# First expert pass of a product-key layer: 112 candidate sums per head for 256, token tiles weighed one by one, one-hot batches over experts 33 to 116

## The reference

```python
q = (xt @ w_query).reshape(n, 8, 2, 128)              # 8 heads, 2 halves
s = jnp.einsum('nhpd,hpkd->nhpk', q, sub_keys)        # 128 keys per half
s1, i1 = lax.top_k(s[:, :, 0], 16)
s2, i2 = lax.top_k(s[:, :, 1], 16)
cand = (s1[..., :, None] + s2[..., None, :])          # 16 x 16 sums per head
cidx = (i1[..., :, None] * 128 + i2[..., None, :])
top, pos = lax.top_k(cand, 16)                        # 16 experts per head
gates = jax.nn.softmax(top)
act = gelu(x . expert_u[e]);  y = sum(gate * act * expert_v[e])
```

## Time and profile before

| | |
|---|---|
| median of 3 runs (lowest, highest) | 1992.9 us (1984.32, 1996.92) |
| profiled execution: time, span | 1994.66 us, 1992.9 us |
| mean granted TensorE clock | 0.952 |
| busy: PE, PEld, DVE, ACT, POOL | 1835.5, 1774.0, 1564.3, 650.6, 931.9 us |
| first pass, L1137: 3072 matmuls | 686.4 to 1388.6 |
| second pass, L1157: 3072 matmuls | 1391.2 to 1971.0 |
| second-level search on DVE begins | 704.3 |
| first gather, last dot | 740.0, 1384.0 |
| first and last matmul of the gate batches | 1004.8, 1311.3 |
| HBM read, written | 361.28 MB, 62.06 MB |

### The profile page before, as it was taken

One profiled execution on the slowest core, in us unless ns is written; L12 is line 12 of the kernel. 1 busy time (PEld: TensorE's weight loads), 2 busy tenths in 40 slices (PEclk: granted clock), 3 DMA queues, 4 the chain that ended last, 5 costly groups with the idle time before them and its releaser, 6 DMA issues.

```text
span 1992.9 us, 29861 instructions
## 1 busy us (share of the span) xinstructions
PE 1835.5 (92%) x11654; PEld 1774.0 (89%) x11654; DVE 1564.3 (78%) x2754; ACT 650.6 (33%) x1037; POOL 931.9 (47%) x676
## 2 busy tenths in 40 slices
PE   5999567887989999999889999997999999999998
PEld 4999566765989999899889999997999999999997
DVE  4797777755459989999899999944788888888852
ACT  4443211112133332222333434432333333333332
POOL 2899897000000258788756566665133334333200
PEclk9999698865989999999999999998999999999999
DMA  7221100001552258787569999999899999999841
GB/s 203 70 77 51 37 1 0 1 1 39 151 170 75 71 173 286 249 275 268 199 205 303 305 304 297 302 333 384 293 364 395 346 364 351 354 344 363 316 172 35
DMA packets 192957, 424.87 MB, mean 213 GB/s; under 512 B 11236, under 2 KB 119296, under 8 KB 184617
## 3 DMA queue, kind: packets, MB, share of 16 engines
q1 hardware_dynamic: 155505, 287.99, 41.9%
q0 software_dynamic: 37312, 134.97, 19.5%
HBM read 361.28 MB, written 62.06 MB: 212 GB/s over the span
## 4 chain that ended last, share of the span: by engine, by line
PE 64%; DVE 26%; issue 3%; DMA 2%; POOL 2%; ACT 2%; SPq 0%; DVEq 0%; ACTq 0%
PE psum L1157 29%; PE psum L1137 14%; PE psum L827 7%; PE psum L1125 4%; PE psum L822 3%; PE psum L915 2%; DMA rowg<-in_expert_u_rows,idx 2%; DVE sel L1938 1%; DVE eqa L1935 1%; DVE junk L1960 1%; DVE cT L1611 1%; DVE besti L1887 1%; DVE WR L1540 1%; DVE sring L1891 1%; PE psum L973 1%
## 5 line engine op out<-in xcount | busy, mean ns | idle before, releaser
L1137 PE MATMUL psum<-xT,WS 128*128 128x416 f32 x3072 | 607.4, 357 | 21.8 <-POOL WS L764 21.4
L1137 PEld LDWEIGHTS psum<-xT,WS 128*128 128x128 f32 x3072 | 580.1, 191 | 30.7 <-POOL WS L764 25.1
L1157 PE MATMUL psum<-AR,WS 128*128 128x416 f32 x3072 | 579.8, 351 | 2.6 <-DVE AR L2048 2.6
L1157 PEld LDWEIGHTS psum<-AR,WS 128*128 128x128 f32 x3072 | 575.0, 188 | 7.5 <-DVE AR L2048 3.0
L764 POOL TENSOR_TENSOR WS<-RAWP,WS 128x1024 fp32r<-128x1024 f32 x128 | 311.7, 2437 | 496.9 <-ACT WS L1438 495.9
L757 POOL DMA_INDIRECT rowg<-in_expert_v,idx x128 | 177.5, 1386 | 315.2 <-DVE acc L1973 305.6
L827 PE MATMUL psum<-xT,WR 128*128 128x280 f32 (+1 forms) x1968 | 261.3, 296 | 2.7 <-DVE xT L1566 2.7
L827 PEld LDWEIGHTS psum<-xT,WR 128*128 128x128 f32 x1968 | 258.4, 193 | 3.4 <-DVE xT L1566 3.2
L1448 ACT ACTIVATE WS<-RAWP 128x1024 fp32r<-128x1024 f32 x128 | 135.8, 1061 | 348.1 <-PE psum L1157 335.5
L2041 DVE TENSOR_TENSOR WS<-RAWP,WS 128x1024 fp32r<-128x1024 f32 x128 | 156.6, 1224 | 117.6 <-ACT WS L1448 117.6
L1475 ACT ACTIVATE actA<-psum 128x416 f32<-128x416 f32 x128 | 66.3, 518 | 447.8 <-PE psum L1137 411.9
(11 more groups left out here) (326 smaller groups left out, 1937.9 us busy)
## 6 DMA issues: line engine op xcount, KB each, us to landing
RAWP<-in_expert_u SPq DMA_DIRECT2D x64, 1024.0 KB
RAWP<-in_expert_v SPq DMA_DIRECT2D x64, 1024.0 KB
act_dram<-actA SPq DMA_DIRECT2D x128, 208.0 KB
gate_dram<-gblk SPq DMA_DIRECT2D x13, 2048.0 KB, 11.9
Gt<-gate_dram SPq DMA_DIRECT2D x32, 832.0 KB
act<-act_dram SPq DMA_DIRECT2D x64, 416.0 KB
RAW<-in_w_in SPq DMA_DIRECT2D x8, 1024.0 KB, 5.4
RAW<-in_w_query SPq DMA_DIRECT2D x8, 1024.0 KB, 5.6
```

The costliest lines, as they stand in the source:

```text
L1137: last = mm(bank[e % 2][:, 0:TD], ws(e)[:, pw, kt * P:(kt + 1) * P], xT[:, px, kt, TSP:TPE], start=(kt == 0 and i == 0), stop=(kt == KT - ...
L1157: last = mm(bank[dt][:, 0:TD], ws(NK + e)[:, pw, dt * P:(dt + 1) * P], AR[:, e % 4, pa, :], start=(e == 0 and i == 0), stop=(e == NK - 1 a ...
```

## The change

The candidates: the best 4 keys of the first half are still summed with all 16 of the second; the other 12 only with the best 4 of the second half, 64 + 48 = 112 sums, since a pair (a, b) can be among the 16 best only if (a + 1)(b + 1) is at most 16. The keys of the picks are found otherwise: the position is turned into an ordinal for each half, compared (greater or equal) with the first ordinal of each of 16 keys, times the step from key to key, and added up in a tree, all in bf16, both halves at once. Its temporaries move: `eqa` into columns of `xT` that the first pass does not read, `sel` into `wrow` (so that the last norm's weights are loaded in the second pass), `stepb` and `topa` into old masks.

Order: tiles 0, 1 and 2 are searched before the batches; tiles 3 and 4 one piece per batch in batches 0 to 17. Each tile is weighed and transposed by itself, through PSUM bank 7; gates use three banks for four. Batch b stands behind step 33 + 83 b // 51 (33 to 116). Dots: 16 before the batches, 100 along them, 12 behind. Gathers begin at step 19 and end with one per step. Gate blocks have 16 tokens for 32, gates are loaded for 8 experts at a time for 4, Gelu's output has four buffers for two, and `yo` and `sq2` lie where `rowg` was.

```diff
-GB = 32
+GB = 16
+GE = 8
-EXP_S_AT, EXP_D_AT = 10, 57
-PAIR_AT = {58 + i: 1 + i for i in range(ND)}
-GATE_AT = {62 + b: b for b in range(NBAT)}
-GSTORE_AT = {62 + 4 * blk + 5: blk for blk in range(NGB)}
-G2_AT = 121
-L2DOTS = 48
+GATE0, GATE_END = 33, 116
+def gate_at(b):
+    return GATE0 + (GATE_END - GATE0) * b // (NBAT - 1)
+GATE_AT = {gate_at(b): b for b in range(NBAT)}
+PAIR_AT = {GATE0 - 4: 1, gate_at(5): 2, gate_at(17): 3, gate_at(28): 4}
+EXP_AT = {17: 0, GATE0 - 8: 1, GATE0 - 2: 2, gate_at(10): 3, gate_at(21): 4}
+WEIGH_AT = {2: 2, 14: 3, 25: 4}
+PAIRS_AT = {8: 2, 20: 3, 32: 4}
+GSTORE_AT = {gate_at(GB // OHB * (blk + 1) - 1) + 2: blk for blk in range(NGB)}
+G2_AT = GATE_END + 7
+DOTS_PRE, DOTS_IN = 16, 100
+def dots_by(b):
+    return DOTS_PRE + DOTS_IN * (b + 1) // NBAT
 GATHER_AT = {}
 for _s in range(PAIRS):
...
+    if _s < DOTS_PRE + 4:
+        _n = 19 + max(_s - 3, 0)
+    elif _s < DOTS_PRE + DOTS_IN + 4:
+        _n = gate_at(min(b for b in range(NBAT) if dots_by(b) > _s - 4)) + 2
     else:
-        _n = 119 + (_s - (L2DOTS + 8 + NBAT)) // 3
+        _n = GATE_END + 3 + (_s - DOTS_PRE - DOTS_IN - 4)
-AX_START, AX_END = 8, 112
+AX_START, AX_END = 5, 112
+GBANKS = 3
...
-        actA = place("actA", [P, 2, TD], region="p")
+        actA = place("actA", [P, 4, TD], region="p")
-        junk = place("junk", [P, 2, D], BF16, region="p")
+        junk = place("junk", [P, D], BF16, region="p")
...
+                else:
+                    V.wait(pe, "pairT", t - 1)
+                V.wait(pe, "gates", t)
...
-                    if g >= 4:
-                        pe.wait_ge(gate_bank, g - 3)
+                    if g >= GBANKS:
+                        pe.wait_ge(gate_bank, g - GBANKS + 1)
...
+                chain(dve.tensor_copy(bb, besti[0:n, t]))
+                op(dve.tensor_copy(sb[:, :, 0, :], bb[:, :, 0:1].to_broadcast([n, 2 * PH, 2])))
+                op(tt(sb[:, :, 1:, :], bb[:, :, 1:].unsqueeze(3).to_broadcast(wide),
+                      bb[:, :, 0:TOPK - 1].unsqueeze(3).to_broadcast(wide), ALU.subtract))
+                at_ = 0
+                op(sums(0, WIDE, TOPK))
+                at_ = WIDE * TOPK
+                chain(sums(WIDE, TOPK, NARROW))
                 yield
...
+                chain(tt(ev.rearrange("p (h x) a r -> p h x a r", x=2),
+                         topb[0:n].rearrange("p (h x) r -> p h x r", x=2).unsqueeze(3).to_broadcast(all_),
+                         firsts[0:n].unsqueeze(1).to_broadcast(all_), ALU.is_ge))
+                yield
+                e2 = ev.rearrange("p c a (r j) -> p c a r j", j=2)
+                chain(tt(e2, e2, sb.unsqueeze(3).to_broadcast([n, 2 * PH, TOPK, TOPK // 2, 2]), ALU.mult))
+                yield
+                for m, a_, b_ in ((8, ev, lv), (4, lv, ev), (2, ev, lv)):
+                    a2 = a_[:, :, 0:2 * m, :].rearrange("p c (a two) r -> p c a two r", two=2)
+                    chain(tt(b_[:, :, 0:m, :], a2[:, :, :, 0, :], a2[:, :, :, 1, :], ALU.add))
...
             def dot(s_):
 
                 dve.wait_ge(rowg_in[s_ % 4], 16 * (s_ // 4 + 1))
-                if s_ >= 2:
-                    dve.wait_ge(dot_done, s_ - 1)
+                if s_:
+                    dve.wait_ge(dot_done, s_)
...
-            for t in range(1, NTP):
-                for _ in level_two(t):
+            for i, _ in enumerate(level_two(1)):
+                if i in (4, 6, 8):
                     next_dot()
...
+            for i, _ in enumerate(level_two(2)):
                 next_dot()
+                if i == 5:
+                    weigh(0)
+                    weigh(1)
+            next_dot()
+            next_dot()
+            pair_values(1)
+            later = (None for t in range(3, NTP) for _ in level_two(t))
             for b in range(NBAT):
+                if b in WEIGH_AT:
+                    weigh(WEIGH_AT[b])
+                if b in PAIRS_AT:
+                    pair_values(PAIRS_AT[b])
+                one_hots(b)
+                while issued[0] < dots_by(b):
+                    next_dot()
+                next(later, None)
+            for _ in range(PAIRS - dots_by(NBAT - 1)):
                 next_dot()
```

More of the change, by code:

```diff
@@ L58 @@
 DB = TD // ND
+WIDE, NARROW = 4, 4
+NCAND = WIDE * TOPK + (TOPK - WIDE) * NARROW
+assert all((a + 1) * (NARROW + 1) > TOPK for a in range(WIDE, TOPK))
 NTP = 1 + ND
@@ L168, in build @@
         ident = place("ident", [P, P])
+        w_tri = used["all"]
         tri = place("tri", [P, P])
@@ L329, in build @@
         s_mm, gelu_done = sem("s_mm"), sem("gelu_done")
-        act_out = [sem(f"act_out{i}") for i in range(2)]
+        act_out = [sem(f"act_out{i}") for i in range(4)]
         rowg_in = [sem(f"rowg_in{i}") for i in range(4)]
@@ L1953, in _, with pair_values, by_batch, twice @@
-            dots = iter(range(PAIRS))
+                chain(tt(gv, gv, gs.unsqueeze(2).to_broadcast([n, PH, TOPK]), ALU.mult), "gates", t)
+            def pair_values(t):
+                T.wait(dve, "pairT", t)
+                b_ = bank[7]
+                g_ = b_[:, 2 * DB:3 * DB]
+                nb_ = DB // OHB
+                pv = pairs[:, (t - 1) * nb_:t * nb_]
+                def by_batch(v):
+                    return v.rearrange("p (b i) -> p b i", i=OHB)
+                def twice(v):
+                    return by_batch(v).unsqueeze(3).to_broadcast([P, nb_, OHB, 2])
+                for x in range(2):
+                    op(dve.tensor_copy(pv[:, :, x], twice(b_[:, x * DB:(x + 1) * DB])))
+                chain(dve.tensor_copy(pv[:, :, 2], twice(g_)))
+                chain(tt(by_batch(gtmp[:, 0]), by_batch(g_), pv[:, :, 2, :, 0], ALU.subtract), "pairT", t)
+                chain(dve.tensor_copy(pv[:, :, 3], twice(gtmp[:, 0])))
+                chain(tt(by_batch(gtmp[:, 1]), by_batch(gtmp[:, 0]), pv[:, :, 3, :, 0], ALU.subtract))
+                chain(dve.tensor_copy(pv[:, :, 4], twice(gtmp[:, 1])))
@@ new lines, in one_hots, with by_two, per_token @@
+            def one_hots(b):
+                i = b % 2
+                def by_two(m):
+                    return m.rearrange("p t (k j) -> p t k j", j=2)
+                def per_token(x):
+                    return pairs[:, b, x].unsqueeze(2).to_broadcast([P, OHB, NK // 2, 2])
+                keys_ = iotab[:].rearrange("p (k j) -> p k j", j=2).unsqueeze(1).to_broadcast(
+                    [P, OHB, NK // 2, 2])
+                if b >= 2:
+                    dve.wait_ge(gate_mm, 2 * b - 2)
+                op(tt(by_two(oh[:, i, 0]), keys_, per_token(0), ALU.is_equal))
+                chain(tt(by_two(oh[:, i, 1]), keys_, per_token(1), ALU.is_equal))
+                for x in range(3):
+                    last = tt(by_two(ohg[:, i, x]), by_two(oh[:, i, 1]), per_token(2 + x), ALU.mult)
+                last.then_inc(oh_ready, 1)
@@ L1963, in next_dot @@
             def next_dot():
-                for s_ in dots:
-                    dot(s_)
-                    return
+                dot(issued[0])
+                issued[0] += 1
             def axpy(s_):
```

191 lines of the change are left out of this document (79 added, 112 removed).

## The result

The changed kernel takes 2029.5 us (median of 4, 2028.0 to 2032.5) against 1991.4 for the kernel before beside it: 1.0196 times as long, 95% interval 1.0169 to 1.0223. The profiled execution took 2029.0 us, its span 2027.2. The forecast of 1969 and its range up to 2003 are wrong; what happened is nearest to the rival in which every low half blocks in full, at 2028.

A forecast was written before the change was run, and what follows sets the result against it. TensorE's waits in the first expert pass, for POOL's low halves and VectorE, were taken as the bound, 46 us winnable. Savings 21 + 5 + 10 less 10 lost make 26 us off 1994.7: 1969, range 1947 to 2003 (own range 1961 to 1978).

The forecast's parts named there:

- the rival in which every low half blocks in full: Batches: each low half costs VectorE 2.41 us, lag 43, ending at 2028; slower than before, chance 0.12.
- The stages that can be won: First pass: 46 us can be won, 25 lost up to 1000, 6.6 up to 1312, 13 in the last part.
- the pace of TensorE: First pass: 4.56 us per plain step, 5.95 with a batch; 147 us from batch 0 to batch 17.
- The search's price: Second-level search on VectorE: 19.2 us a tile, 2.13 per piece, against 34 unhindered; its compare near 2.2 us.
- The early part: First pass up to 1000: 4 of 25 us lost remain, 21 saved; VectorE idles some 30 us without cost to TensorE.
- The end: Last steps of the first pass: one gather a step instead of three; 3 of 13 us kept, 10 saved.
- The second pass: Second pass over the experts: 580 us, unchanged by larger gate loads and axpys spread over more steps.
- the price s of a low half: VectorE time lost per low half in the batches: taken as 1.1 us, bounds 0 and 2.41.
- The batches: One-hot batches: 5.43 us each plus 2.13 of search in the first 18; lag 8, then 2, 10 us lost.
- an interpolation over the share of two-input work: Batches: from 0.7 at a quarter two-input work and 1.67 at 73%, 1.1 us per low half at 55%.
- the lockstep: Earlier trace's one-hot stage: VectorE held by POOL's half, 1.67 us each; rival at that price 1986, chance 0.22.
- The rival about gathers: Batches: gathers block too, 0.95 us each, s effectively 2.2, end some 2010; counted within the slower rival's 0.12.

The follow-up runs named there:

- experiment 2: Changed kernel with gathers from the 21st on two steps later in POOL's queue (offset 4 for 2), the last ones two per step: 1987.4 us.
- experiment 6: New search in the old order, all tiles searched first: five operations per batch 2021.4 us; two operations 1968.0; five operations with gathers one step later 1975.0.
- experiment 7: Kernel before the change, with gathers of the one-hot stage three steps earlier in POOL's queue: 2026.5 us.
- (3): Changed kernel without the first pass's row gathers from the 21st on, that part of the output not computed: 1992.6 us (one run).
- (1): Changed kernel with a batch's five one-hot operations made two (both compares in one, three products in one): 2004.0 us.
- (8): Changed kernel with gathers from the 21st on one step later in POOL's queue (offset 3): 2003.4 us.
- (5): Changed kernel with two one-hot operations and gathers two steps later: 1973.8 us; tile 3 also searched ahead: 1975.6; with four dots in that search: 1970.1.
- experiment 4: Changed kernel with POOL's low half made over 64 of 1024 columns from step 4 on, dense output not accurate: 1943.7 us (one run).
- (9): New search, old order, two operations: batches behind steps 55 to 106, 2002.3 us; 54 to 105, 1958.6; then gathers later 1960.1, also five operations 1964.6.

## Why the prediction was wrong

**What it had right.** The stages that can be won and the pace of TensorE: 147 and 302 us measured with short halves, for 147 and 303 worked out. The search's price: 2.29 for 2.2. The early part: 4 us lost for 4; VectorE did idle, 22.7 us. The end: 10 saved was forecast, 13 came. The second pass: unchanged. Together some 42 us were won outside the batches' pace, for the 36 forecast: 46 could be won, and 4 of them were lost again ahead of batch 0. The sign that the prediction named for its slower rival, waits for one-hots to the end of the batches, is what the trace shows.

**The step that failed** is the price s of a low half in "The batches": 1.1 us, from an interpolation over the share of two-input work. From batch 0 to 17, 196.4 = 17 x (7.56 + 1.6 s) + 7.7 gives s = 2.2. From there to the last, 332.7 us less 8.5 for weighing and pair values (estimated as the 7.7 was) is 9.5 a batch, and with 56 steps for 34 batches (9.5 - 5.43) / 1.65 = 2.5, the whole half. The lag so was 49 us at batch 17, not 8, and 31 more after it, not 2: 80 for 10. 80 - 42 = 38, and the first pass is 38.0 us longer.

That the slower rival's 2028 lies so near is in part luck. It put 69 us on the batches and 36 on the gains, where 80 and 42 were measured, and the first pass began 3.7 us earlier; the differences nearly cancel.

**Why the interpolation was wrong.** It took the halves as coming at moments that have nothing to do with VectorE's. I had the price of the worst case right, and gave it 0.12, "against: dots read PSUM and run beside L764". But gathers that wait for dots stood in front of the halves, and I had written as much of the early part. In the batches I costed a gather at nothing, because a gather does not block VectorE. It is what it waits for that matters: it lets the halves go behind the dots, into the one-hots. Moving the gathers alone took 42 us off the changed kernel (experiment 2) and 46 off another (6), and put 35 on the kernel before (7); removing them gave no more (3). That is shown. In the kernel before, with one half and one dot per batch, a gather stood five steps behind the batch with the dot that frees its buffer. The change put it two steps behind, with two gathers per batch; experiment 7 puts it at two as well.

The batches side by side, from TensorE's timelines (us):

| | batches 0 to 17 | 17 to 51 | POOL's wait for dots | time |
|---|---|---|---|---|
| changed kernel | 196.4 | 332.7 | 243 | 2029.5 |
| two operations (1) | 191.9 | 306.9 | 124 | 2004.0 |
| gathers one step later (8) | 190.3 | 308.7 | 90 | 2003.4 |
| gathers two steps later (2) | 180.4 | 304.7 | 39 | 1987.4 |
| both (5) | 168.5 | 302.5 | 32 | 1973.8 |
| both, tile 3 ahead, four dots in it (5) | 153.7 | 302.3 | 34 | 1970.1 |
| short halves (4) | 147.0 | 302.3 | 30 | 1943.7 |

So the gathers' wait accounts for 44 of the 80 us: nearly all that is lost behind batch 17, but only 16 of the 49 ahead of it. With gathers that no longer lead, the same sum gives (180.4 - 7.7) / 17 = 7.56 + 1.6 s, s = 1.6 for the first 18 batches: the price of the lockstep, and still not 1.1. So with five operations the interpolation was too low there even out of the bad phase.

**The part that five operations have.** Two operations in place of five save 25 us (1) and 53 us (6) in kernels whose gathers lead with five; where they do not, 14 (5 against 2) and 4 (9). Part of the saving is a change of phase. In experiment 6 POOL's wait for dots falls from 203 to 39 us, and the 52 batches take 305 us from first to last for 358, as they do when the gathers are moved instead (306). So the 53 and the 46 are two ways out of one bad phase and not two costs. That a shorter run has fewer gaps for a half, and ends early enough for the gather to find its dot done, fits the timelines but was not tested by itself. I had priced five operations as in the earlier trace rows and not asked this.

**The rival about gathers.** Beside gathers the one-hot operations took 0.68 us after the change too, so gathers do not block them; with short halves all 80 us go. My rival, that gathers might block as well and make s 2.2, gave nearly the right size of s for the wrong reason. The page on GpSimd ("GPSIMD Engine Reference", 1. Specifications, the Trainium skill) names two-input VectorE operations as contending, and experiment 4 agrees for POOL's tensor operation.

**Still open.** With later gathers the first 18 batches still take 180 us for 147. All of it goes when POOL's halves are short, so it is the same contention. Two operations take 12 us off it, and tile 3 searched ahead another 15; what the last 7 come from, the search pieces of tile 4, weighings or pair values, was not settled. Nor was a way found to search tile 3 ahead without the 9 us or more by which batch 0 then came later. Batches put one per step behind the whole search (9) ran at TensorE's pace, and the kernel takes 15 us less than the kernel with both remedies (1958.6 for 1973.8).

## What to carry to other kernels

When two engines take turns at something, the mean price of a meeting says little: ask what releases each one's operation, because a wait on the other engine can tie the two together, in the good phase or in the bad one, for as long as the loop runs. When a remedy does not move the total, look at the stage that it was meant for: the gain may be there, and lost again elsewhere. Look at what stands in an in-order queue in front of an operation that nobody seems to wait for. And when a schedule shifts by one step, check which transfers of other queues it now shares a step with.

## What the runs showed of the hardware that was not expected

- In the timelines shown, a POOL tensor operation that is due gets in between back-to-back VectorE operations with two SBUF inputs. Two due ones run through together (4.75 us), and a product of 0.68 us took 5.51 us, waiting for both.
- The exclusion works the other way too, as in the earlier trace rows: beside a VectorE operation of 3072 columns a gather issue of 0.95 us took 2.29 us, while such operations of 1024 columns took their 0.68 us beside a gather.
- SP's issue of a DMA is no constant. For a 208 KB store it took 0.32 us when weight load and gate store alternated (none of 42 between 1000 and 1250 us above 0.72), but more than 1 us in 15 of 36, and up to 5.00 us, when both 1 MB transfers were issued in one step.
